# Convolution taps that read the gate in PSUM, and norm operands in PSUM, in a two-block fp32 transformer kernel

## The reference, cut to what matters

```
def conv_ffn(h, w_up, conv_w, conv_b, w_down, rows, cols):
    val, gate = jnp.split(h @ w_up, 2, axis=-1)
    gate = depthwise_conv_grid(gate, conv_w, conv_b, rows, cols)   # 3 x 3, 'SAME', per channel
    return (jax.nn.gelu(gate, approximate=False) * val) @ w_down
```

## Time and profile before

| | us |
|---|---|
| median of 3 runs (3427.71 to 3432.18) | 3428.41 |
| span of the profiled execution, first to last instruction | 3432.9 |
| PE busy | 3148.7 (92%) |
| DVE busy | 1876.7 (55%) |
| POOL busy | 1920.5 (56%) |
| ACT busy | 714.1 (21%) |

### The profile page before, as it was taken

How to read it: one execution, slowest core, us unless ns; L and a number is a source line. 1 busy time by engine, 2 the same in 40 slices (tenths; PEclk the granted TensorE clock), 3 DMA queues, 4 the chain that set the end, 5 groups by cost and what they waited for, 6 DMA issues and landing times.

```text
span 3432.9 us, 37709 instructions
## 1 busy us (share of the span) xinstructions
PE 3148.7 (92%) x13568; PEld 2514.2 (73%) x13568; DVE 1876.7 (55%) x1942; ACT 714.1 (21%) x1200; POOL 1920.5 (56%) x1030
## 2 busy tenths in 40 slices
PE   6878899987898887899999999999999999789998
PEld 3666547866676676688887888888788887668886
DVE  7876762378868488632253722256732258863223
ACT  3245451121101233221112211110111113321110
POOL 4321205655555465576665666666666666557664
PEclk9988899999999898999999999999999999899999
DMA  6600003222222222222232222222222222222221
GB/s 235 240 25 31 31 1 100 97 74 68 68 86 74 68 86 78 76 98 98 98 104 86 92 93 98 98 92 98 92 98 97 93 98 88 78 77 95 98 98 67
DMA packets 86011, 306.69 MB, mean 89 GB/s; under 512 B 9553, under 2 KB 10065, under 8 KB 85633
## 3 DMA queue, kind: packets, MB, share of 16 engines
q1 hardware_dynamic: 82512, 297.73, 25.5%
q10 hardware_dynamic: 3376, 7.24, 0.6%
HBM read 302.84 MB, written 2.10 MB: 89 GB/s over the span
## 4 chain that ended last, share of the span: by engine, by line
PE 69%; DVE 24%; issue 3%; ACT 3%; SPq 1%; DMA 0%; DVEq 0%; ACTq 0%
PE acc L1483 64%; DVE ff_conv L1364 6%; DVE rec_rec_x L1873 2%; DVE rec_rec_in L1902 2%; DVE rec_rec_u L1915 1%; PE side L724 1%; DVE ff_conv L1362 1%; DVE ff_lo L1373 1%; DVE square_sum L1817 1%; DVE ada_more L1098 1%; PE acc L702 1%; DVE state L1244 1%; SPq L494 0%; DMA xc<-in_ctx 0%; DVE rec_rec_in L1900 0%
## 5 line engine op out<-in xcount | busy, mean ns | idle before, releaser
L1446 POOL TENSOR_TENSOR w_lo<-w_raw,w_hi 128x1024 fp32r<-128x1024 f32 x513 | 1250.0, 2437 | 1443.4 <-PE acc L1483 1396.1
L1483 PE MATMUL acc<-h_hi,w_hi 128*128 128x512 f32 x2224 | 892.8, 401 | 127.9 <-DVE ff_hid L1370 47.3
L1483 PE MATMUL acc<-h_lo,w_hi 128*128 128x512 f32 x2224 | 880.9, 396 | 0.0
L1483 PE MATMUL acc<-h_hi,w_lo 128*128 128x512 f32 x2224 | 879.5, 395 | 0.0
L1436 POOL TENSOR_SCALAR w_hi<-w_raw 128x1024 fp32r<-128x1024 f32 x513 | 687.4, 1340 | 37.3 <-DMA w_raw<-in_weights 37.3
L1483 PEld LDWEIGHTS acc<-h_hi,w_hi 128*128 128x128 f32 x2224 | 425.8, 191 | 245.4 <-DVE ff_hid L1370 54.1
L1483 PEld LDWEIGHTS acc<-h_hi,w_lo 128*128 128x128 f32 x2224 | 426.3, 192 | 88.3
L1483 PEld LDWEIGHTS acc<-h_lo,w_hi 128*128 128x128 f32 x2224 | 426.9, 192 | 85.7 <-issue 1.7
L1835 DVE TENSOR_TENSOR x<-acc,x 128x512 f32 (+1 forms) x160 | 110.6, 691 | 557.6 <-PE acc L1483 557.6
L1483 PE MATMUL acc<-mlp_hid_hi,w_hi 128*128 128x512 f32 x1024 | 398.3, 389 | 0.0
L1483 PE MATMUL acc<-mlp_hid_lo,w_hi 128*128 128x512 f32 x1024 | 398.3, 389 | 0.0
...
## 6 DMA issues: line engine op xcount, KB each, us to landing
...
```

Source lines behind the costliest of these rows:

```text
L1446: pool.tensor_tensor(w_lo[:, slot, :], w_raw[:, slot, :], w_hi[:, slot, :].bitcast(F32), ALU.subtract).then_inc(panel_made, 1)
L1483: ins = pe.matmul(out, lhs, rhs, start=start, stop=stop, skip_group_check=group)
```

## The change

The pad goes. The nine taps read the gate in its PSUM bank; each of the eight outer taps reads and writes only the subrange of the grid that its shift covers (7 or 8 rows of 63 or 64 columns), and the centre tap comes first and writes the whole. The product with the value goes to a PSUM bank that was idle in this stage (`spare_bank`, two banks of `side`) instead of `ff_hid`. DVE's order becomes: taps of tile j, product of tile j-1, low part of tile j-2; ACT's: Gelu of tile j, high part of tile j-1. The gate's bank is now freed by the last tap, not by ACT's copy. For the norms from the third on, in both blocks, the squares go to `spare_bank`; for the first block's last two norms the reciprocal goes to PSUM (`side[:, 0, :]`), and the feed-forward's h is built from one DVE instruction with the gain, one ACT instruction with the shift, and one DVE instruction that adds the shift and subtracts. `gain2` is allocated twice as long, `cnv_p` 14 columns longer.

```diff
@@ -211,7 +211,7 @@
...
-        overlay("conv", cnv_g=([P, 2, T], F32), cnv_x=([P, 2, T], F32), cnv_p=([P, 2, C_TAPS - 1 + T], F32),
+        overlay("conv", cnv_g=([P, 2, T], F32), cnv_x=([P, 2, T], F32), cnv_p=([P, 2, C_TAPS - 1 + T + 14], F32),
                 cnv_c=([P, 2, T], F32), cnv_b=([P, 2, T], F32),
@@ -329,7 +329,7 @@
...
             gain1 = fb("gain1", [P, 2, KT])
-            gain2 = fb("gain2", [P, KT])
+            gain2 = fb("gain2", [P, 2 * KT])
             products = fb("products", [P, 6 * KT, 2])
@@ -395,13 +395,9 @@
...
             with ExitStack() as part:
-                f2_full = fa("f2_full", [P, 2, T])
-                f2_scaled = fa("f2_scaled", [P, 2, T])
                 ff_hi = fa("ff_hi", [P, 2, 8, T], F32R)
                 ff_lo = fa("ff_lo", [P, 2, 8, T], F32R)
-                ff_pad = fa("ff_pad", [P, 2, GRID_H + 2, GRID_W + 2])
                 ff_conv = fa("ff_conv", [P, 2, T])
-                ff_hid = fa("ff_hid", [P, 2, T])
@@ -456,8 +452,6 @@
...
         mg_lo_made = sem("mg_lo_made")
-        pads_made = sem("pads_made")
-        ff_conved = sem("ff_conved")
         ff_gelu = sem("ff_gelu")
@@ -466,6 +460,12 @@
...
             return C if norm == 1 else T
+
+        spare_bank = [side[:, 1, :], side[:, 2, :]]
+
+        def squares(norm, k):
+
+            return square[:, k % 2, 0:sums(norm)] if norm < PE_NORMS else spare_bank[k % 2]
@@ -799,7 +799,7 @@
...
                 w = sums(norm)
-                act.activation(square[:, k % 2, 0:w], src[:, k, 0:w], ACT.Square).then_inc(squared, 1)
+                act.activation(squares(norm, k), src[:, k, 0:w], ACT.Square).then_inc(squared, 1)
@@ -1005,22 +1005,22 @@
...
             root_of(2)
-            modulated(2, 2 * KT, h_hi, f2_scaled, f2_full, lambda k: gain2[:, k:k + 1], lambda k: mod[:, 3 * KT + k, 0:1])
+            for k in range(KT):
+                act.wait_ge(n_scaled_made, 2 * KT + k + 1)
+                act.activation(h_hi[:, k, :], spare_bank[k % 2], ACT.Identity, bias=mod[:, 3 * KT + k, 0:1]).then_inc(h_hi_made, 1)
+
+            def high(group, i):
+                j = FF1_GROUPS[group][i]
+                wait_taken(act, out_ff_up(group) + 2 * i + 1)
+                act.activation(ff_hi[:, group % 2, i, :], spare_bank[j % 2], ACT.Copy).then_inc(ff_hi_made, 1)
...
                 for i, j in enumerate(FF1_GROUPS[group]):
-                    o = out_ff_up(group) + 2 * i
-                    wait_made(act, o)
-                    if j >= 2:
-                        act.wait_ge(ff_conved, j - 1)
-                    else:
-                        act.wait_ge(pads_made, 1)
-                    act.activation(ff_pad[:, j % 2, 1:GRID_H + 1, 1:GRID_W + 1],
-                                   bank(o).rearrange("p (r c) -> p r c", r=GRID_H), ACT.Copy).then_inc(out_taken[o % BANKS], 1)
-                    act.wait_ge(ff_conved, j + 1)
+                    wait_taken(act, out_ff_up(group) + 2 * i)
                     act.activation(ff_conv[:, j % 2, :], ff_conv[:, j % 2, :], ACT.Gelu).then_inc(ff_gelu, 1)
-                    wait_taken(act, o + 1)
-                    act.activation(ff_hi[:, group % 2, i, :], ff_hid[:, j % 2, :], ACT.Copy).then_inc(ff_hi_made, 1)
+                    if i:
+                        high(group, i - 1)
+                high(group, len(FF1_GROUPS[group]) - 1)
             for g in range(3):
@@ -1056,16 +1056,16 @@
...
                         dve.wait_ge(stat_made, norm - PE_NORMS)
-                    dve.tensor_copy(square_sum[:, 0:w], square[:, 0, 0:w]).then_inc(summed, 1)
+                    dve.tensor_copy(square_sum[:, 0:w], squares(norm, k)).then_inc(summed, 1)
                 else:
                     dve.wait_ge(summed, KT * norm + k)
-                    dve.tensor_tensor(square_sum[:, 0:w], square_sum[:, 0:w], square[:, k % 2, 0:w], ALU.add)\
+                    dve.tensor_tensor(square_sum[:, 0:w], squares(norm, k), square_sum[:, 0:w], ALU.add)\
                        .then_inc(summed, 1)
...
                 dve.wait_ge(root_made, norm + 1)
-                own(dve.reciprocal(rstd[:, 0:w], root[:, 0:w]), rstd_made, norm + 1)
+                own(dve.reciprocal(rstd[:, 0:w] if norm < PE_NORMS else side[:, 0, :], root[:, 0:w]), rstd_made, norm + 1)
@@ -1141,7 +1141,7 @@
...
                                    table[:, names["b_ada"] + ADA_FIRST:names["b_ada"] + 6 * KT], ALU.add))
-            own(dve.scalar_tensor_tensor(out=gain2[:, :], in0=mod[:, 4 * KT:5 * KT, 0], scalar=1.0,
+            own(dve.scalar_tensor_tensor(out=gain2[:, 0:KT], in0=mod[:, 4 * KT:5 * KT, 0], scalar=1.0,
                                          in1=table[:, names["norm2"]:names["norm2"] + KT], op0=ALU.add, op1=ALU.mult),
@@ -1346,32 +1346,59 @@
...
             rstd_of(2)
-            modulated(2, 2 * KT, x, h_hi, h_lo, f2_scaled, f2_full)
-            dve.memset(ff_pad[:, :, :, :], 0.0).then_inc(pads_made, 1)
+            for k in range(KT + 1):
+                if k < KT:
+                    if k >= 2:
+                        dve.wait_ge(h_lo_made, 2 * KT + k - 1)
+                    dve.scalar_tensor_tensor(out=spare_bank[k % 2], in0=x[:, k, :], scalar=gain2[:, k:k + 1], in1=side[:, 0, :],
+                                             op0=ALU.mult, op1=ALU.mult).then_inc(n_scaled_made, 1)
+                if k:
+                    dve.wait_ge(h_hi_made, 2 * KT + k)
+                    dve.scalar_tensor_tensor(out=h_lo[:, k - 1, :], in0=spare_bank[(k - 1) % 2], scalar=mod[:, 3 * KT + k - 1, 0:1],
+                                             in1=h_hi[:, k - 1, :].bitcast(F32), op0=ALU.add, op1=ALU.subtract).then_inc(h_lo_made, 1)
+
+            def grid(ap):
+                return ap.rearrange("p (r c) -> p r c", r=GRID_H)
+
+            def convolved(o, j):
+
+                src, conv = grid(bank(o)), grid(ff_conv[:, j % 2, :])
+                wait_made(dve, o)
+                link(dve.tensor_scalar(conv, src, col("conv_w", FF1 * 4 + j), col("conv_b", j), ALU.mult, ALU.add))
+                around = [tap for tap in range(9) if tap != 4]
+                for tap in around:
+                    r, c = tap // 3 - 1, tap % 3 - 1
+                    r0, r1, c0, c1 = max(0, -r), GRID_H - max(0, r), max(0, -c), GRID_W - max(0, c)
+                    out = conv[:, r0:r1, c0:c1]
+                    ins = dve.scalar_tensor_tensor(out=out, in0=src[:, r0 + r:r1 + r, c0 + c:c1 + c],
+                                                   scalar=col("conv_w", FF1 * tap + j), in1=out, op0=ALU.mult, op1=ALU.add)
+                    if tap != around[-1]:
+                        link(ins)
+                take(ins, o)
+
+            def gated(o, j):
+
+                dve.wait_ge(ff_gelu, j + 1)
+                wait_made(dve, o)
+                take(dve.tensor_tensor(spare_bank[j % 2], bank(o), ff_conv[:, j % 2, :], ALU.mult), o)
+
+            def hidden_low(group, i):
+                j = FF1_GROUPS[group][i]
+                dve.wait_ge(ff_hi_made, j + 1)
+                own(dve.tensor_tensor(ff_lo[:, group % 2, i, :], spare_bank[j % 2], ff_hi[:, group % 2, i, :].bitcast(F32),
+                                      ALU.subtract), ff_lo_made, j + 1)
             def up(group):
+                first, n = out_ff_up(group), len(FF1_GROUPS[group])
                 for i, j in enumerate(FF1_GROUPS[group]):
-                    o = out_ff_up(group) + 2 * i
-                    pad, conv = ff_pad[:, j % 2, :, :], ff_conv[:, j % 2, :].rearrange("p (r c) -> p r c", r=GRID_H)
-                    wait_taken(dve, o)
-                    for tap in range(9):
-                        r, c = tap // 3, tap % 3
-                        src = pad[:, r:r + GRID_H, c:c + GRID_W]
-                        w = col("conv_w", FF1 * tap + j)
-                        if tap == 0:
-                            ins = dve.tensor_scalar(conv, src, w, col("conv_b", j), ALU.mult, ALU.add)
-                        else:
-                            ins = dve.scalar_tensor_tensor(out=conv, in0=src, scalar=w, in1=conv, op0=ALU.mult, op1=ALU.add)
-                        if tap < 8:
-                            link(ins)
-                    own(ins, ff_conved, j + 1)
-                    dve.wait_ge(ff_gelu, j + 1)
-                    wait_made(dve, o + 1)
-                    ins = dve.tensor_tensor(ff_hid[:, j % 2, :], bank(o + 1), ff_conv[:, j % 2, :], ALU.mult)
-                    take(ins, o + 1)
-                    dve.wait_ge(ff_hi_made, j + 1)
-                    own(dve.tensor_tensor(ff_lo[:, group % 2, i, :], ff_hid[:, j % 2, :], ff_hi[:, group % 2, i, :].bitcast(F32),
-                                          ALU.subtract), ff_lo_made, j + 1)
+                    convolved(first + 2 * i, j)
+                    if i:
+                        gated(first + 2 * i - 1, j - 1)
+                    if i >= 2:
+                        hidden_low(group, i - 2)
```

(13 more changed lines are left out.)

## The result

The changed kernel takes 3338.52 us (median of 4 runs, 3331.49 to 3338.95) against 3428.06 us (4 runs, 3427.66 to 3432.18): a ratio of 0.9726, 95% interval 0.9712 to 0.9741. It is faster by 89.5 us by the medians; the ratio of 0.9726 stands for 94 us. Forecast were 99.0 us and 3329.4. The two profiled executions have spans of 3432.9 and 3336.4, 96.5 apart: an execution takes 1.8 us more than its span (3338.18 against 3336.4 for the one profiled of after), so the profiled execution of before, some 3434.7, lay 6.6 us above its median, and that of after at its median.

The account below looks back on a forecast made before the run. PE bounds the kernel as a whole, DVE the feed-forward stage. Savings of 84.1 + 2.0 + 6.6 + 1.0 + 3.8 + 1.5 = 99.0 us from 3428.4 gave 3329.4; own range 3320 to 3342, 8 in 10 3317 to 3348.

Parts of the forecast that it names:

- (1): Feed-forward stage: DVE's tile falls below PE's 10.9 us, so PE sets the pace; 84.1 us saved, 3.5 of it alignment.
- (2): Building the feed-forward's h: a shorter chain without two-SBUF-input instructions saves 2.0 us, ends 0 and 4.
- (B): Rival: taps from PSUM cost 1.12 us on average, as from the pad; 3366 if slower, 3380 if blocked; chance 0.07.
- (3): Norms: sums of squares out of POOL's way save 1.1 us at six places, 6.6; first block's last norm 1.0.
- (4): Alignment elsewhere: operands starting on multiples of 64 gain 0.0067 us a matmul; 3.8 for `mg`, `om`/`og`, `cnv`, 1.5 for others.
- (A): Rival: alignment has no effect and the 0.2333 pace has another cause; 3338 us, chance 0.12.
- (C): Rival: PSUM tap reads at an odd column or with a cut row are slow; at 2.0 us each 3531; chance 0.03.
- (D): Rival: PE's new waits for the value's bank, 3.4 us of slack, eat DVE's gain; 3351 at 1 us a tile; chance 0.07.

Follow-up runs that it names:

- e5_taps_only: Kernel before with only the nine taps reading the gate's PSUM bank on cut subranges; old order, product in SBUF, norms unchanged: 3349.89 us, ratio 0.9760.
- e6_order_only: Kernel before with only the new DVE and ACT order, the pad kept and copied one tile ahead: 3416.49 us, ratio 0.9943.
- e2_all128: Changed kernel with 128 bytes more in `gain2` and 128 more ahead of `cnv_hi`: 3334.17 us, ratio 0.9711.
- e8_more_dve: Changed kernel with five more unused DVE operations a tile, from the gate's PSUM bank: 3359.35 us, ratio 0.9784.

## Why the prediction was right, and where it was wrong

**(1) The stage: right.** From norm to norm the feed-forward lost 461.8 - 378.4 = 83.4 us. Terms (1) and (2) gave 86.1, of which 3.5 were the alignment; without it 82.6. The reason stands too: DVE's instructions with two SBUF inputs queued behind POOL's, and with the first input in PSUM they don't (`e5_taps_only`: nothing but that, 79.3 us). That the taps merely fell at other times than POOL's work is ruled out: before, 24 of the 176 taps began during a `w_lo`, and each took 2.76 to 2.94 us; after, 88 began during one, and each took 0.675 to 0.685. The tap was taken as 0.75; it is 0.695 in the mean, since the cut subranges of 441 to 504 columns save what they leave out. The forecast's period, 10.9, and PE at 1.00 came as written.

What the forecast didn't say is that the new order is not needed. It counted 1.52 us of round trips among what DVE saves; with taps from PSUM they lie in time in which DVE waits for PE anyway, and the chain's bound is PE. As a part of a sum that ends at PE's pace this did no harm, but it doesn't tell a reader which half to build. Rival (B)'s working used the same number by itself, 22 x 1.52 = 33.4 us for the stage, and `e6_order_only` shows 18.0. Its average tap of 1.12 us was also read from one tile, gaps included; over all 176 the mean is 1.19.

**(2) Building h: right, mis-sized.** 2.0 were taken, with an upper end of 4. It gave 4.0 (19.2 to 15.2 us). The period of the new chain is 1.44 us a tile (the forecast had 1.55), so the stretch from the scale of tile 3 on went from 11.5 to 8.0 us, where 8.5 were forecast. The two losses that the forecast took off didn't come: the tiles before gained 0.5 instead of losing 0.4, and PE begins 0.06 us after the last low part, as before.

**(3) The norms: right.** 1.1 a place were taken and 6.6 for six; it is 1.26 and 7.6. The first block's last norm gave 0.6 of the 1.0 taken. The block moved to the low part of tile 6 (1.52 before, 2.12 after) and ended in time, as the forecast had it.

**(4) Alignment: wrong.** The step that failed is "The operands with 0.2267 start on a multiple of 64. The longer `gain2` (64 bytes) and `cnv_p` (4224) put all of them there. I take 0.0067 us a matmul as gained." The observation of two paces was right, and so was that the cause is a start address. The rule was the simplest that separates the rows at hand, and the recurrent mixer spoke against it: its operands start 192 bytes past a multiple of 256, on a multiple of 64, and run at 0.2293, between the two paces; no row of it was read. Shown in place of it: the pace goes by the distance to the weights modulo 256, and 0 is the fast one: 0.2267, where 96 and 128 have 0.2333. Three terms hung on this step, 3.5 + 3.8 + 1.5 = 8.8 us. Rival (A), which said that the alignment would have no effect and gave 3338, describes the result; with the right distance the feed-forward's part is there after all (`e2_all128`: 3.55 of the 3.5 forecast), and 1.0 of the 1.3 of `cnv`, in the stretch of its mixer. The page "SBUF — State Buffer" of the Trainium skill (Door 1: The DMA port swizzle) counts in lines of 16 bytes, by which no shift by a multiple of 32 would change anything; the paddings of the change, which moved `ff` by 32 bytes and `cnv` by 96, changed nothing, and the 128 bytes more of `e2_all128` took 0.0067 us off a matmul, so the measurement decides against it here.

**The rivals.** (B) and (C) fall with one line, 675/682/744 ns for 176 taps: not blocked, and not slower for an odd first column or a row cut to 63. "VectorE: DVE Perf Modes" of the Trainium skill (Rules for kernel authors) says to copy to SBUF first if many operations follow. Nine follow here, and the copy was the costly choice: 1.19 against 0.695 us a tap in the mean. Even without GpSimd the copy would gain nothing for these fp32 operations: the shortest tap from SBUF took 750 ns, and `gated_add`, of the same form and with an input in PSUM, 749 to 752. (D) falls with the waits: PE waits nowhere for the product in the trace of after; it does in `e8_more_dve` (15.8 us in 18 waits), where DVE's tile is longer than PE's.

**Span and median.** By the traces the forecast was 99.0 and the saving 96.5. The 8.8 of (4) are missing; 2.0 more came from (2) and 3.4 more after the fourth norm (11.0 against 7.6), 2.1 lie ahead of the third norm, where the paces are the same and executions differ, and 0.9 went at the stage's end, from the last add to the reciprocal (1082.52 to 1087.59, before 1168.87 to 1173.08); the rest, 0.3, is in (1). Of the 3.4 only 0.6 are the norms'; about 2 lie in the recurrent mixer's stretch, which varies by itself, so the sum came near in part by luck. By the medians the saving is 89.5, since the profiled execution of before was a long one by 6.6 us; the forecast had found 4.5 of this and taken the saving as independent of it. So of the error of 9.1 us in the time 2.5 are the difference of the traces, misses and luck together, and 6.6 come from the profiled execution of before. The time lies inside the forecast's own range, 3320 to 3342, but where the prediction had put rival (A). The low end of that range isn't worked out cleanly: the upper ends are 2, 2.4, 1.2 and 2.5 above what was taken, 8.1 and not 9.
